# One token-mixer layer with a mixture of experts on one core: the SSM branch's projections and its scan put into one block, with the early chunk states among the gate-z items

## The chip, the cores and the metric

The kernel runs on one core of a Trainium2 chip, as one launch. The metric is the device time in microseconds. The kernel before was timed in three runs: 2568.36, 2576.6 and 2577.54 us, median 2576.6. One further execution was profiled; the rows below come from it.

## The reference, cut to what matters

The layer modulates its input, projects it into four branches, merges them behind gates, and ends with a mixture of experts. The change touches the second branch, a state-space model (SSD) with 12 heads in 4 groups, over 1024 tokens in 8 chunks of 128, plus 256 context tokens in 2 chunks, in both directions:

```
z, xbc, dt = split(p_b)                        # 768, 1792 and 24 columns of u @ w_in
xs, b_in, c_out = split(silu(conv3(xbc)))      # 768, 4 x 128, 4 x 128
dt = softplus(dt + bias);  log_decay = -dt * exp(a_log)
a_cum = cumsum(log_decay) in each chunk
decay_to_end = exp(a_cum[-1] - a_cum)
state[c] = sum_l b_in[l] * decay_to_end[l] * (xs*dt)[l]       # one per chunk and direction
h[c+1] = exp(a_cum[-1]) * h[c] + state[c]                     # the context's states start it
y = (c_out b_in^T * decay) (xs*dt) + c_out h[c] * exp(a_cum) + ssd_d * xs
y = rms_norm(y * silu(z))
```

Eleven of the chunk states are called early: four of the two context chunks (both directions), which give the initial states, and seven of the forward direction. The scan proper then walks the chunks from the last to the first, forms the backward states on its way, and writes y.

## The kernel before, in words

The program is a row of stages; each is one block in which the five engines run their own instruction lists and meet through semaphores, and each ends in a barrier of all engines (`stage`, line 361). `ssd_scan_stages` (L944) runs two of them, `stage_ssd_project` (L956) and `stage_scan` (L1302). A tensor `merged` serves as scratch in the first, and holds the forward states and then y in the second.

**Projections.** 21 items stream through a ring of four weight buffers: item 0 gives the raw dt, items 1 to 14 the xbc channels, items 15 to 20 the gate z, 128 channels each. For each item ScalarE rounds the weights and VectorE forms the remainder (`split_weights`, L924: L937 and L940). TensorE then runs `project`: 48 matmuls of 512 columns (L390; three products for each of 8 slices of the contraction and 2 halves of the tokens), into PSUM banks 0 and 1 for even items, 3 and 4 for odd ones; items up to 10 also do the context, into bank 2 or 5. After project(m), TensorE transposes the tile of item m-1 to token order (`turn`, L1112, banks 6 and 7), ScalarE evicts that (L1141), and POOL stores it to HBM: xs and b to `xbc_tok`, z to `z_tok` (L1039). b and c go out by channel as well (`xbc_chan`, L1287), and the cumulative sums to `cum_rows` (L1291). SP's queue carries the ring's loads, and behind them the stores of the last two z items. The block ends when every store has landed.

**Scan.** SP loads xs and b of each early state from `xbc_tok` (L1376, L1377), in four buffers; POOL multiplies xs by dt_to_end (L1403, "ending"); TensorE forms the state in 4 products of 192 columns (`chunk_state`, L1439; 8 records in the trace) into banks 3 and 4 or 5 and 6 in turn; VectorE decays the running state (L1566) and adds the new one (L1569). Then TensorE starts on chunk 7: `segments` (L1460, L1461; six for each chunk, banks 0, 1 and 7) give the exponents, ScalarE takes their exponentials (`grow`, L1537), VectorE mixes them with the scores of b and c (L1576, L1581), and TensorE sums skip term (L1474), diagonal term (L1482) and the states' products (`states_out`, L1468, banks 5 and 6). Each chunk also forms the backward state that the next one needs.

What sets the order: each engine's list is in program order, and a wait holds everything behind it. POOL's and SP's transfers are issued in that order too.

Of the kernel before, what the change touches and what calls it, by code (L numbers as in the profile page):

```python
# [943 lines left out]
def ssd_scan_stages(k, merged):  # L944


    with ExitStack() as ctx:
        sb = k.resident(ctx)
        n = CHUNKS + CTX_CHUNKS
        dt = {name: sb("dt_" + name, [P, n, 2, HEADS]) for name in  # L950
              ("exp_cum", "dt_to_end", "total", "bias")}
        stage_ssd_project(k, dt, merged)
        stage_scan(k, dt, merged)


def stage_ssd_project(k, dt, scratch):  # L956

# [9 lines left out]
    n = CHUNKS + CTX_CHUNKS  # L967
# [12 lines left out]
    with k.stage("xbc") as (sb, sem):  # L980
        turned = sb("turned", [P, 2, n, P])
        upper = sb("upper", [P, 2, KT * P], F32R)
        uc = sb("uc", [P, KT, CTX])
        uc_rest = twin(nc, "xbc_uc", [P, KT, CTX])
        uc_upper = sb("uc_upper", [P, KT, CTX], F32R)
        raw = sb("raw", [H2, n * P])
        bias, a_log = sb("bias", [P, H2]), sb("a_log", [P, H2])
        tmp, neg = sb("tmp", [P, n, H2]), sb("neg", [P, n, H2])
        step, log_decay, log_step, to_end, cum = (sb(x, [P, n, 2, HEADS]) for x in (
            "step", "log_decay", "log_step", "to_end", "cum"))  # L990
        cum_up, cum_lo = sb("cum_up", [CUMS, 2, P], F32R), sb("cum_lo", [CUMS, 2, P], F32R)
# [12 lines left out]
        def banks(m):  # L1004
            return 3 * (m % 2)

# [20 lines left out]
        def wide(row):  # L1027
            return row[:, :].unsqueeze(1).broadcast_to([P, n, H2])
# [4 lines left out]
        def chunks_of(v):  # L1033
            return v.rearrange("p (c h) -> p c h", c=n)
# [7 lines left out]
        raw_turned_at = ps[:, 6, 0:n * H2]  # L1042
        cum_at = [ps[:, 7, d * n * HEADS:(d + 1) * n * HEADS] for d in range(2)]
        total_at = ps[:, 7, n * H2:2 * n * H2]

        with nc.Block() as block:
            @block.sync
            def _(sp):
                sp.dma_start(uc[:, :, :], a["ctxT"].rearrange("(k p) t -> p k t", p=P)).then_inc(uc_in, 16)
                sp.dma_start(bias[:, :], k.row("dt_bias")).then_inc(small_in, 16)  # L1050
                sp.dma_start(a_log[:, :], k.row("a_log")).then_inc(small_in, 16)
                ring.stream(sp)
# [9 lines left out]
            def _(pe):  # L1062
# [18 lines left out]
                def turn_raw():  # L1081
                    pe.wait_ge(raw_ready, 2)
                    for c in range(n):
# [18 lines left out]
                def turn(m):  # L1102
# [8 lines left out]
                    for c in range(CHUNKS):  # L1111
                        mm = nc.tensor.transpose(ps[:, 6 + c // 4, (c % 4) * P:(c % 4 + 1) * P],  # L1112
                                                 shaped[:, m % 2, c * P:(c + 1) * P], k.const("ident"))
# [6 lines left out]

                for m in range(items):
# [9 lines left out]
                turn(items - 1)  # L1131

            @block.scalar
            def _(act):
# [39 lines left out]
                for m in range(1, items):  # L1174
# [26 lines left out]
                    else:  # L1201
                        free_shaped(m)
                        nc.scalar.activation(shaped[:, b, 0:T], both, ACT.Silu).then_inc(shaped_ready, 1)
# [4 lines left out]
                        if turns(m - 1):  # L1208
                            evacuate_turned(m - 1)
                evacuate_turned(items - 1)  # L1210

            @block.vector
            def _(v):
# [42 lines left out]

                for m in range(1, items):
                    if is_conv(m):
                        convolve(m)
                    if m + 2 < items:  # L1260
# [19 lines left out]
                ch.wait()  # L1280

            @block.gpsimd
            def _(pool):
                for m in range(1, items - 2):
                    if 6 < m <= convs:
                        pool.wait_ge(shaped_ready, m)
                        pool.dma_start(a["xbc_chan"][m - 7], shaped[:, m % 2, 0:T]).then_inc(chan_out[m % 2], 16)  # L1287
                    if m == turning + 3:
                        pool.wait_ge(cum_split, 2)
# [2073 lines left out]
```

## Time and profile before

| | |
|---|---|
| median of three timed runs | 2576.6 us (2568.36 to 2577.54) |
| profiled execution | 2572.02 us, span 2570.2 us |
| busy share of the span | PE 94%, PE weight loads 76%, DVE 63%, ACT 37%, POOL 10% |
| mean granted TensorE clock | 0.968 |
| projections of the SSM branch | 491 to about 792 us of the span |
| seam up to the first segments matmul | about 792 to 837 us |
| scan proper | 837 to 938 us |

PE is TensorE's matmuls, PEld its weight loads, DVE VectorE, ACT ScalarE, POOL GpSimd, SPq the transfers that SyncE issues. L1112 is line 1112 of the kernel before. A share is a mean over stages with different limits; the chain of waits of the whole execution holds only its last instruction, so the seam is read from the stretches and the timeline.

### The profile page before, as it was taken

The numbers are of one execution on the slowest core, as the hardware profiler recorded it, in microseconds if no ns is written. First come the engines' busy times: TensorE is split into PE (matmuls) and PEld (weight loads), VectorE is DVE, ScalarE is ACT, GpSimd is POOL, SyncE is SP. The second block draws the span as 40 slices with busy tenths as digits, with TensorE's granted clock in tenths as the row PEclk, the third lists the DMA queues.
The fourth block names the chain that finished last, engine by engine and source line by source line (L and its number), as shares of the span: only waits on it lengthen the run. The fifth ranks groups of instructions, "written<-read, shape, count | busy, mean of one in ns | idle before, by whom it ended". The sixth has DMA issues, their size and how long they took to land. (4 is left out here: it accounts for less than half of the span.)

```text
span 2570.2 us, 30487 instructions
## 1 busy us (share of the span) xinstructions
PE 2407.5 (94%) x11928; PEld 1950.9 (76%) x11928; DVE 1630.3 (63%) x1666; ACT 941.3 (37%) x1100; POOL 251.7 (10%) x234
## 2 busy tenths in 40 slices
PE   6999899799996989999999999999599999999994
PEld 2468778678885878788877888868588888888882
DVE  6453299533323763522984635668888889888976
ACT  5233301333321533101112100021277777777764
POOL 0000000000103310000000001100011212121210
PEclk8999999899998999999999999999799999999997
DMA  5431255212326222111111113533689999999975
GB/s 202 169 115 50 74 173 178 85 54 82 123 69 195 88 64 98 61 49 51 46 41 45 37 49 130 198 142 130 259 316 368 365 363 363 363 371 387 384 269 204
DMA packets 95120, 437.51 MB, mean 170 GB/s; under 512 B 16057, under 2 KB 28617, under 8 KB 80299
## 3 DMA queue, kind: packets, MB, share of 16 engines
q1 hardware_dynamic: 68330, 357.81, 37.5%
q0 software_dynamic: 26688, 78.30, 8.7%
q8 instruction: 70, 1.15, 0.2%
q14 instruction: 32, 0.25, 0.0%
HBM read 401.51 MB, written 55.51 MB: 178 GB/s over the span
## 5 line engine op out<-in xcount | busy, mean ns | idle before, releaser
L390 PE MATMUL ps<-uT_upper_rest,ring_rest 128*128 128x512 f32 x1296 | 513.0, 396 | 0.0
L390 PE MATMUL ps<-uT_upper_rest,mix_upper 128*128 128x512 f32 x768 | 307.6, 400 | 9.6 <-DVE mix_val L2342 5.3
L390 PE MATMUL ps<-uT_rest,mix_upper 128*128 128x512 f32 x768 | 306.5, 399 | 0.0
L390 PEld LDWEIGHTS ps<-uT_upper_rest,ring_rest 128*128 128x128 f32 x1296 | 244.8, 189 | 61.5
L390 PEld LDWEIGHTS ps<-uT_upper_rest,mix_upper 128*128 128x128 f32 x768 | 145.7, 190 | 47.1 <-DVE mix_val L2342 5.7
L390 PEld LDWEIGHTS ps<-uT_rest,mix_upper 128*128 128x128 f32 x768 | 145.7, 190 | 32.6 <-issue 0.5
L1774 ACT ACTIVATE mix_gates<-ps 128x1024 f32<-128x1024 f32 x24 | 24.7, 1027 | 384.3 <-PE ps L390 367.1
L1825 DVE TENSOR_TENSOR mix_prod<-mix_gates,ps 128x1024 f32<-128x1024 f32 x24 | 29.3, 1220 | 209.9 <-PE ps L390 209.9
L2873 PE MATMUL ps<-ex_u_raw_rest,uT_rest 128*128 128x256 f32 x560 | 157.5, 281 | 0.0
L390 PE MATMUL ps<-uT_upper_rest,xbc_upper 128*128 128x512 f32 x336 | 136.6, 407 | 7.6 <-DVE ring_rest L940 7.6
L2871 PE MATMUL ps<-ring_rest,uT_rest 128*128 128x256 f32 (+1 forms) x416 | 135.5, 326 | 3.1 <-DVE uT_rest L3236 2.4
L2871 PE MATMUL ps<-ex_upper,uT_rest 128*128 128x256 f32 (+1 forms) x424 | 135.4, 319 | 0.0
L390 PE MATMUL ps<-uT_rest,xbc_upper 128*128 128x512 f32 x336 | 135.0, 402 | 0.0
L2872 PE MATMUL ps<-ex_upper,uT_rest 128*128 128x256 f32 (+1 forms) x424 | 134.3, 317 | 0.0
L2872 PE MATMUL ps<-ring_rest,uT_rest 128*128 128x256 f32 (+1 forms) x416 | 133.5, 321 | 0.0
L2761 POOL DMA_INDIRECT y_rows<-sb_uT,ex_scatter_at x35 | 92.1, 2630 | 293.4 <-ACT sb_uT L2990 293.1
L390 PE MATMUL ps<-mix_y_upper,mix_upper 128*128 128x512 f32 x288 | 114.6, 398 | 1.8 <-DVE mix_y_bT_rest L398 1.8
L390 PE MATMUL ps<-mix_y_upper,ring_rest 128*128 128x512 f32 x288 | 112.3, 390 | 0.0
L2873 PE MATMUL ps<-uT_upper_rest,uT_rest 128*128 128x512 f32 x280 | 110.8, 396 | 0.0
L2873 PE MATMUL ps<-merged_rest,ex_hid_up 128*128 128x512 f32 x280 | 110.2, 394 | 0.0
L2873 PEld LDWEIGHTS ps<-ex_u_raw_rest,uT_rest 128*128 128x128 f32 x560 | 105.4, 188 | 0.0
L2357 DVE SCALAR_TENSOR_TENSOR mix_y_aT<-mix_val,sb_cols,mix_y_aT 128x64 f32<-128x64 f32 (+14 forms) x120 | 90.2, 752 | 4.1
(464 smaller groups left out, 5535.7 us busy)
## 6 DMA issues: line engine op xcount, KB each, us to landing
sb_spare<-in_ex_g SPq DMA_DIRECT2D x35, 2048.0 KB, 9.9
ex_u_raw<-in_ex_u SPq DMA_DIRECT2D x35, 2048.0 KB, 10.2
sb_merged<-in_ex_d SPq DMA_DIRECT2D x35, 2048.0 KB, 9.3
ring<-in_conv SPq DMA_DIRECT2D x32, 512.0 KB, 3.3
ring<-in_w_gate SPq DMA_DIRECT2D x32, 512.0 KB, 3.3
mix_piece<-in_w_late POOLq DMA_DIRECT2D x32, 512.0 KB, 5.4
ring<-in_w_ssd SPq DMA_DIRECT2D x21, 512.0 KB, 3.2
ring<-in_w_mod SPq DMA_DIRECT2D x16, 512.0 KB, 4.2
```

The source lines that it names most:

```text
L390: last = self.nc.tensor.matmul(out, weight, x[:, k, lo:hi], start=(k == 0 and n == 0), stop=(k == kt - 1 and n == 2))
L1774: nc.scalar.activation(gate_of(i), both(gate_bank(i)), ACT.Sigmoid).then_inc(gate_ready, 1)
L1825: nc.vector.tensor_tensor(mine if first else prod[:, :], gate_of(i), both(gate_bank(i) + 2), ALU.mult).then_inc(prod_ready, 1)
L2357: ins = nc.vector.scalar_tensor_tensor(out=acc[:, lo:hi], in0=val[:, t, lo + s * GRID_W:hi + s * GRID_W], scalar=weight, in1=acc[:, lo:hi] ...
L2761: pool.indirect_dma_start(out=a["y_rows"], out_offset=bass.IndirectOffsetOnAxis(scatter_at[:, i:i + 1], 0), in_=y, in_offset=None, bounds_ ...
L2871: nc.tensor.matmul(out, left_up, w_up, start=first, stop=False)
L2872: nc.tensor.matmul(out, left_lo, w_up, start=False, stop=False)
L2873: return nc.tensor.matmul(out, left_up, w_lo, start=False, stop=last)
```

## The change

The two stages become one, `stage_ssd`, with one block. Its tiles lie at chosen byte offsets of one arena of 73,344 bytes a partition, because the scan's tiles now exist beside those of the projections: tiles of the scan lie over tiles that an earlier step has done with, and waits guard the reuse. The silu of z goes to a tile of its own, since the scratch is wanted for states. `grow_b` and `off` lie partly over `turned`, from which the z stores read.

The eleven early states run inside the z items, two in each of items 15 to 19 and one in item 20 (`early_at`), in banks 2 and 5, which only items with context use. There is one pair of banks and two buffers for the loads, in place of two pairs and four. TensorE runs the first of a pair between project(m) and the turn, the second behind the turn. VectorE reads the two halves by two instructions. POOL, no longer SP, issues the loads of the early states, of chunk 7 (`state_first`) and of its b and c (`out_first`).

In chunk 0 of the scan (n = 0), ScalarE's fifth `grow`, VectorE's second `take_off` and POOL's skip product wait for `last_out`, the stores of the last two z items. SP loads chunk n = 1 and on, behind those stores. Exp's table is loaded between ScalarE's last two evictions. The scan's loop is otherwise the same.

```diff
+    FIRST = 11
+    ARENA = 73344
+        def shaped_of(m):
+            return shaped[:, m % 2, 0:T] if is_conv(m) else shaped_z[:, m % 2, :]
...
+        grow_f, grow_b = at_byte("grow_f", 0, [P, 2, HEADS, P]), at_byte("grow_b", 12288, [P, HEADS, P])
+        off, skip = at_byte("off", 18432, [P, SSD_D]), at_byte("skip", 21504, [P, SSD_D])
+        xs, xend = at_byte("xs", late, [P, 2, SSD_D]), at_byte("xend", late + 6144, [P, 2, SSD_D])
...
+        def early_sum(h):
+            return ps[:, 2 + 3 * h, 0:half]
+
+        def early_at(m):
+
+            return range(max(2 * (m - convs - 1), 0), min(2 * (m - convs), FIRST))
...
             @block.sync
...
+                for n in range(1, CHUNKS):
+                    if n == 1:
+                        sp.wait_ge(state_mm, last_early(1) + 1)
+                        chan_done(sp)
+                    else:
+                        sp.wait_ge(y_done, n - 1)
+                    load_state(sp, n % 2, chunk(n), in_state[n % 2])
+                    load_out(sp, n, in_out[n % 2])
...
             @block.tensor
...
+                def early_state(m):
+                    if m:
+                        pe.wait_ge(state_read, 2 * m)
+                    pe.wait_ge(in_early[m % 2], 32 * (m // 2 + 1))
+                    chunk_state(m, m % 2, early_sum)
                 for m in range(items):
                     project(m)
...
+                    for e in early_at(m)[:1]:
+                        early_state(e)
                     if m >= 2 and turns(m - 1):
                         turn(m - 1)
+                    for e in early_at(m)[1:]:
+                        early_state(e)
                 pe.wait_ge(ring.freed, ring.done(base + items - 1))
                 pe.sem_inc(ring.freed, full - items)
                 turn(items - 1)
...
+                pe.wait_ge(rounded, 4)
+                segments(0, 0)
+                segments(0, 1)
+                pe.wait_ge(turned_ready, reads_until(items - 1) + 2)
+                segments(0, 2)
+                forward_out(0)
...
             @block.scalar
...
+                nc.scalar.preload_act_table(ACT.Exp)
                 evacuate_turned(items - 1)
+                act.wait_ge(dt_ready, 1)
+
+                def grow(n, u):
+                    act.wait_ge(seg_mm, 6 * n + u + 1)
+                    if n == 0 and u == 4:
+                        act.wait_ge(last_out, 32)
...
             @block.vector
...
+                def early_state(m):
...
+                    v.wait_ge(state_mm, m + 1)
+                    for h in range(2):
+                        tt(as_halves(new)[:, h, :], as_halves(new)[:, h, :], early_sum(h), ALU.add).then_inc(state_read, 1)
+                    v.wait_ge(state_read, 2 * (m + 1))
...
                 for m in range(1, items):
                     if is_conv(m):
                         convolve(m)
+                    for e in early_at(m):
+                        early_state(e)
+                    if m == convs + 2:
+                        prepare()
                     if m + 2 < items:
                         split_weights(k, None, v, base, m + 2, upper, cast, w_split)
...
+                    take_off(n, 0, state_in(c))
+                    mix(n, 0)
+                    if n:
+                        take_diagonal(n - 1)
+                    if n == 0:
+                        v.wait_ge(last_out, 32)
+                    take_off(n, 1, off[:, :])
...
             @block.gpsimd
...
+                def early_ready(m):
+
+                    for e in early_at(m):
+                        if e >= 2:
+                            pool.wait_ge(state_mm, e - 1)
+                        load_state(pool, e % 2, early[e][1], in_early[e % 2])
+                    for e in early_at(m):
+                        pool.wait_ge(in_early[e % 2], 32 * (e // 2 + 1))
+                        ending(e % 2, early[e][1], early[e][0])
...
                     elif convs < m < items - 2:
+                        early_ready(m + 1)
                         store_z(pool, m, tok_out[turn_no(m) % 2])
+                    if m == turning + 3:
+                        pool.wait_ge(dt_ready, 1)
+                        for b in range(2):
+                            pool.wait_ge(tok_out[b], 16 * (turning // 2))
+                        early_ready(convs + 1)
+                    if m == convs + 1:
+                        chan_done(pool)
+                        load_out(pool, 0, out_first)
+                        pool.wait_ge(blank, 1)
+                        load_rows(0, 0)
+                        load_rows(0, 1)
+                early_ready(items - 1)
+                pool.wait_ge(state_mm, FIRST)
+                load_state(pool, 0, chunk(0), state_first)
...
+                    else:
+                        pool.wait_ge(d_in, 16)
+                        pool.wait_ge(last_out, 32)
```

## Rows read from the trace of the kernel before

**Rows 1.** Stretches: us, then each engine's busy time, granted clock, DMA share, GB/s.

```profile
779.00:792.00 13.00, 13.00 (x64) 10.64 (x63) 0.00 (x0) 2.41 (x4) 0.89 (x1) 1.00 0.14 40
792.00:798.00 6.00, 1.60 (x13) 1.15 (x11) 0.00 (x0) 2.87 (x5) 0.00 (x0) 1.00 0.81 237
798.00:804.00 6.00, 0.00 (x0) 0.00 (x0) 0.11 (x1) 0.14 (x1) 0.00 (x0) 0.51 0.64 200
804.00:810.80 6.80, 0.00 (x0) 0.00 (x0) 2.05 (x3) 1.64 (x3) 1.47 (x1) 0.50 0.74 243
810.80:837.00 26.20, 18.50 (x88) 15.93 (x88) 21.19 (x21) 0.00 (x0) 18.38 (x12) 0.92 0.90 297
```

**Rows 2.** Timeline of PE over the seam: start, duration, instruction, idle before and releaser.

```profile
791.49 1.04 PE L1112 MATMUL ps<-sb_consts,sb_merged 128*128 128x128 f32 x8
794.10 1.06 PE L1112 MATMUL ps<-sb_consts,sb_merged 128*128 128x128 f32 x8 [1.57 <-ACT xbc_turned L1141]
810.86 5.03 PE L1439 MATMUL ps<-scan_xend,scan_b_tok 128*128 128x192 f32 x16 [15.69 <-POOL scan_xend L1403]
...
837.31 0.36 PE L1460 MATMUL ps<-scan_never,scan_eye 128*128 128x256 f32 x1 [2.60 <-DMA scan_rows<-cum_rows]
...
838.82 1.47 PE L1468 MATMUL ps<-sb_merged,scan_c_chan 128*128 128x192 f32 x8
```

**Rows 3.** Timeline of PE, one z item earlier: turn and next projection.

```profile
779.42 1.03 PE L1112 MATMUL ps<-sb_consts,sb_merged 128*128 128x128 f32 x8
780.21 0.48 PE L390 MATMUL ps<-uT_upper_rest,xbc_upper 128*128 128x512 f32 x1
```

**Rows 4.** Timelines of DVE and POOL in the z items.

```profile
769.82 1.23 DVE L940 TENSOR_TENSOR ring_rest<-ring,xbc_upper 128x1024 fp32r<-128x1024 f32 x1 [10.85 <-ACT xbc_upper L937]
782.18 0.89 POOL L1039 DMA_DIRECT2D z_tok<-xbc_turned  x1 [10.23 <-ACT xbc_turned L1141]
```

**Rows 5.** Timelines of DVE and PE: evictions, and a chunk state inside the scan.

```profile
703.88 0.41 DVE L1273 CAST xbc_cum_up<-ps 96x256 fp32r<-96x256 f32 x1
...
846.02 1.52 PE L1439 MATMUL ps<-scan_xend,scan_b_tok 128*128 128x192 f32 x8
847.24 0.41 PE L1460 MATMUL ps<-scan_never,scan_eye 128*128 128x256 f32 x1
847.65 0.95 DVE L1612 TENSOR_TENSOR scan_state_b<-scan_state_b,ps 128x768 f32<-128x768 f32 x1 [1.21 <-PE ps L1439]
```

**Rows 6.** A POOL transfer, POOL's products (min/median/max ns), landing of b.

```profile
715.72 0.53 POOL L1287 DMA_DIRECT2D xbc_chan<-sb_merged  x1 [10.86 <-ACT sb_merged L1199]
...
L1403 POOL TENSOR_TENSOR scan_xend<-scan_xs,sb_dt_dt_to_end x13: 1462/1470/2181, 809.2 to 917.1; 128x768 f32<-128x768 f32 x13
...
DMA to landing us min/median/max: 3.3/3.7/6.2
```

**Rows 7.** ACT's last eviction and table load; the last z stores, and their landing.

```profile
795.20 1.07 ACT L1141 COPY xbc_turned<-ps 128x512 f32<-128x512 f32 x2 [1.25 <-PE ps L1112]
...
804.38 1.28 ACT L1537 ACT_TABLE_LOAD   x1
...
793.98 2.69 SPq L1039 DMA_DIRECT2D z_tok<-xbc_turned  x2
...
z_tok<-xbc_turned SPq DMA_DIRECT2D x2, 512.0 KB, 6.8
```

**Rows 8.** Chunk 0 of the scan: POOL's skip product, PE's use of it.

```profile
839.84 1.50 POOL L1427 TENSOR_TENSOR scan_skip<-scan_xs,scan_d_row 128x768 f32<-128x768 f32 x1
843.74 0.81 PE L1474 MATMUL ps<-scan_skip,sb_consts 128*128 128x384 f32 x2
```

**Rows 9.** The stage after: a stretch at the lower clock, and two matmuls in it.

```profile
941.00:944.50 3.50, 3.29 (x8) 2.62 (x9) 3.43 (x6) 0.00 (x0) 0.00 (x0) 0.50 0.30 102
...
942.23 0.63 PE L390 MATMUL ps<-uT_upper_rest,ring_rest 128*128 128x512 f32 x1
942.65 0.63 PE L390 MATMUL ps<-uT_upper_rest,mix_upper 128*128 128x512 f32 x1
```

More of the change, by code:

```diff
@@ L1027, in wide @@
         def wide(row):
-            return row[:, :].unsqueeze(1).broadcast_to([P, n, H2])
+            return row[:, :].unsqueeze(1).broadcast_to([P, n_all, H2])
         def heads(v):
@@ new lines, in halves, with as_halves, last_early, chan_done @@
+        def halves(first_bank):
+            return ps[:, first_bank:first_bank + 2, 0:half]
+        def as_halves(v):
+            return v.rearrange("p (b n) -> p b n", b=2)
+        def last_early(b):
+            return max(m for m in range(FIRST) if m % 2 == b)
+        def early_sum(h):
+            return ps[:, 2 + 3 * h, 0:half]
+        def early_at(m):
+            return range(max(2 * (m - convs - 1), 0), min(2 * (m - convs), FIRST))
+        def chan_done(eng):
+            for b in range(2):
+                eng.wait_ge(chan_out[b], 16 * sum(q % 2 == b for q in range(7, convs + 1)))
@@ new lines, in load_state, with load_out @@
+        def load_state(eng, b, c, landed):
+            eng.dma_start(xs[:, b, :], a["xbc_tok"][c, :, 0:SSD_D]).then_inc(landed, 16)
+            eng.dma_start(b_tok[:, b, :], a["xbc_tok"][c, :, SSD_D:SSD_D + GROUPS * P]).then_inc(landed, 16)
+        def load_out(eng, n, landed):
+            c = chunk(n)
+            for q, dst in enumerate((b_chan, c_chan)):
+                src = a["xbc_chan"][GROUPS * q:GROUPS * (q + 1), :, c * P:(c + 1) * P]
+                eng.dma_start(dst[:, n % 2, :, :], src.rearrange("g p t -> p g t")).then_inc(landed, 16)
@@ L1131, in _, with segments @@
                 turn(items - 1)
+                def segments(n, u):
+                    at_bank = SEG[(6 * n + u) % 3]
+                    if 6 * n + u >= 3:
+                        pe.wait_ge(grown, 6 * n + u - 2)
+                    pe.wait_ge(in_rows[u // 3], 16 * (n + 1))
+                    for d in range(2):
+                        out = ps[:, at_bank, d * PAIR:(d + 1) * PAIR]
+                        nc.tensor.matmul(out, eye[:, :], never[:, d, :], start=True, stop=False)
+                        mm = nc.tensor.matmul(out, ones[:, :], rows[:, d, u * PAIR:(u + 1) * PAIR], start=False, stop=True)
+                    mm.then_inc(seg_mm, 1)
@@ new lines, in states_out, with skipped @@
+                def states_out(n, d):
+                    b = n % 2
+                    state = state_in(chunk(n)) if d == 0 else state_b[:, b, :]
+                    for g in range(GROUPS):
+                        mm = nc.tensor.matmul(ps[:, 5 + g // 2, (g % 2) * 192:(g % 2 + 1) * 192],
+                                              c_chan[:, b, g, :], state[:, g * 192:(g + 1) * 192], start=True, stop=True)
+                    mm.then_inc(off_mm, 1)
+                def skipped(n, q):
+                    pe.wait_ge(skip_ready, n + 1)
+                    nc.tensor.matmul(ps[:, 3 + q, 0:half], k.const("ident"), skip[:, q * half:(q + 1) * half],
+                                     start=True, stop=False)
@@ new lines, in diagonal @@
+                def diagonal(n, q):
+                    pe.wait_ge(mixed, 2 * n + q + 1)
+                    pe.wait_ge(in_state[n % 2] if n else state_first, 32 * max((n + 1) // 2, 1))
+                    for e in range(6):
+                        h = 6 * q + e
+                        mm = nc.tensor.matmul(ps[:, 3 + q, e * HD:(e + 1) * HD], grow_f[:, n % 2, h, :],
+                                              xs[:, n % 2, h * HD:(h + 1) * HD], start=False, stop=(e == 5))
+                    mm.then_inc(diag_mm, 1)
@@ L1571, in _ @@
+                        ch.wait()
+                        v.sem_inc(dt_ready, 1)
                 v.sem_inc(state_done, 1)
```

460 lines of the change are left out of this document (184 added, 276 removed).

## The prediction

> **What bounds the kernel now.** I read the stretches first (busy time of every engine and the clock granted to TensorE, stretch by stretch), because the page's share of 94% for PE is a mean over stages. In the seam between projections and scan that share collapses: 13.0 us of 13.0 while the last gate-z items run, then 1.60 of 6.0, 0 of 6.0, 0 of 6.8, and 18.50 of 26.2 [rows 1]. The timeline of PE names the events. The last projection gives way to the turn of z item 19 at 791.49, item 20's turn starts at 794.10, the first early chunk state at 810.86, and the scan proper (the segments matmul) only at 837.31 [rows 2]. So 45.8 us lie between the end of the projections and the scan, with 20.1 us of PE work in them. Inside the z items PE is saturated and the others wait: one item costs 12.07 us, of which its turn costs 0.79 [rows 2, 3], while DVE stood idle 10.85 us before its one split and POOL 10.23 us before its one store [rows 4]. The early states would lie beside idle engines, but on the engine that has no idle.
>
> **The change part by part.** Let T be the end of a z projection.
>
> *PE work moved into the z items.* An early chunk state occupies PE's queue for 1.22 us (846.02 to 847.24), its last result comes out at 847.54 and DVE starts on it at 847.65 [rows 5]. All eleven now use one pair of banks, so the next one waits until DVE has read both halves. No row has a 384-column eviction; 256 columns took 0.41 us and 768 took 0.95 [rows 5], so I estimate 0.55 each, 1.1 for the two, and the next state starts 2.8 us after the one before. Items 16 to 19 put a turn into that gap: 2.8 + 1.22 = 4.0 us, less the 0.8 for the turn which was there before, is 3.2 us each, 12.8 together. Item 15 has no turn in the gap: 4.0. Item 20 has one state: 1.2. Sum 18.0 us. If the gap cost nothing it would be 11 x 1.22 = 13.4; I keep that as the low end.
>
> *Does POOL deliver in time?* POOL must store z item m-1, issue four loads, and form two products before T of the next item. From T: first state and turn 2.0, eviction of the turn some 1.5 more, so the store starts at T + 3.6. Then 0.9 for the store [rows 4] and 4 x 0.55 for the loads (POOL issued a plain transfer of 128 rows in 0.53 [rows 6]), landing 3.7 us after issue (SP's loads of the same rows; POOL's own have no row yet), products 1.47 each [rows 6]: the first is ready about T + 10.8, the second T + 12.3. PE asks for them at T + 15.2 and T + 18.0. With the worst rows (0.89 an issue, landing 6.2, product 2.18) it is about T + 14.7 and T + 16.8, still in time. One item is tighter: on item 16 POOL also loads the first b and c blocks, waits for DVE to clear the rows tile and issues two row loads, some 4 us more. Mean rows still fit, the worst rows cost about 4 us. I take zero and keep 7 us (this item, and one us for each of three others) as the high end. DVE's added work, some 4 us of 15 per item, lies before its next weight split, which PE needs an item later; cover gone, each us would be a us. The ring's loads stay on SP's queue; the early loads add 640 KB a state, about 87 GB/s over a 15 us item, where the seam ran 237 GB/s and more [rows 1].
>
> *The end of the z phase.* With 18.0 us more, item 19's turn starts at 809.5 and item 20's at 812.1; the first two segments follow at once, at 812.9. Before, this was 837.31: a lead of 24.4. The third segment needs the bank of item 20's turn. ScalarE evicted that one from 795.20 [rows 7], now 813.2; the activation table load of 1.28 us [rows 7] is put between its two evictions, where ScalarE waited for PE 1.25 us anyway, so the eviction ends at 814.4 (0.1 late). The first forward product follows at 814.9 against 838.82 [rows 2]: the lead is 23.9.
>
> The Trainium skill, "ScalarE: Activation LUTs", section "What ACT_TABLE_LOAD costs", adds a drain of about 1.38 us to each switch; by it the eviction and the rest would come 1.4 us later and the gain would be 18.1 instead of 19.5. No row separates such a drain.
>
> *The wait that replaces the barrier.* The tiles of the scan now share bytes with the buffer from which z is stored, so ScalarE's fifth pair of growth factors, DVE's second off-diagonal product and POOL's skip product of chunk 0 wait until the last two z stores have landed. Behind POOL's wait stand the skip product, the next end product and a row load; PE waits for the first two. Before, the two stores were issued from 793.98 to 796.67 and took 6.8 us [rows 7], and the barrier opened right behind them. Now the second goes out at 814.4; 6.8 makes 821.2, and I add 1.5 (an estimate) because the loads of chunk 7 and 6 share the DMA engines: 822.7. The skip product (1.50 [rows 8]) ends at 824.2. PE used it at 843.74 [rows 8], 19.5 us later. The end product follows by 1.5, at 825.7, and PE comes to the state that needs it 2.28 us after the skip (843.74 to 846.02 [rows 5, 8]), at 826.5: no further loss. From here the eight chunks run as before, since their code and waits are the same. The loads of chunk 6, which went out well ahead before, now go out behind the z store at about 815 and land some 6 us later; they are wanted about 828. The lead that counts is therefore **19.5 us**. If the stores land in 3.8 us, the lead stays 23.9; 4 us later than I take, it is 15.5.
>
> What else changes (arrays laid over each other, more semaphores cleared at the stage's end, two small ScalarE copies on item 16) lies beside PE or is below 1 us; the clear I bound by 0 and 1.
>
> **The sum.** The profiled execution took 2572.0 us; less 19.5 it is 2552.5. The median shown is 2576.6, 4.6 above it, and the three runs (2568.4 to 2577.5) lie on both sides, so I go half way: **2555 us**. Its own range: a z phase longer by only 13.4 would give a lead of 24.1, a landing 4 us later 15.5, the clear one less, 14.5. From a base of 2574.5, give or take 2.3, that is 2548 to 2562.
>
> **The rivals.**
>
> *POOL is late: the early states do not hide.* POOL's queue is in order, and each pair of loads waits behind a store that itself waits for PE. For it: in the seam PE waited 15.69 us for POOL's first product [rows 2], and everything now sits in this queue. Against: over 4 us of slack by typical rows. With 7 us lost, the lead is 12.5 and the time 2562; with landings still slower (10 us each pair) it loses 4 us an item, about 20, and nothing is left: 2574. Range of this rival 2562 to 2574. One way to get there: products took up to 2.18 us beside DVE instead of 1.47 [rows 6]; if the store, the two loads and the product ahead of a first state each waited out one DVE instruction of 1.23 us [rows 4], that state would be ready at T + 15.7, half a us late, 2 us over four items. The Trainium skill, "SBUF — State Buffer", section "SBUF: two separate sides", gives the rule for it: GpSimd, which also writes the descriptors of POOL's transfers, is locked out for the whole of a DVE instruction in a two-port mode or with two SBUF inputs. The trace agrees for the products; for transfers no row shows it. It is why this case has more than a tenth.
>
> *The seam's wait is bigger than the barrier was.* Here it decides only how much is gained: a landing 12 us after issue, at 826.4, ends the skip product at 827.9, a lead of 15.8 and 2559. It is inside the forecast's range.
>
> *TensorE's clock falls in the z items; slower.* Today the z items run unbroken at 1.00. The seam shows 0.51 and 0.50 after PE had stopped [rows 1], the lower of the two levels (1.2 and 2.4 GHz). At that level (granted 0.50 in 941.0 to 944.5) one 512-column matmul follows another after 0.42 us (942.23 to 942.65 [rows 9]) against 0.235 (12.07 less 0.79 us for the 48 of an item [rows 2, 3]): 9 us an item. The breaks that I forecast are 0.8 us, in item 15 1.6. If they pull the clock down, the five items behind cost 45 us more and the time is 2600; the point from which the change loses is a little over two items at the low clock. Against: with PE busy 1.60 us of 6 the granted clock was still 1.00 [rows 1]. The Trainium skill names this pattern in "TensorE: Matmul & The Clock Gate", section "HAM oscillation — how this bites in real kernels": waits between bursts of matmuls re-throttle the array. The row of 792 to 798 does not bear it out for breaks this short.
>
> **How the numbers follow.** Forecast 0.72, POOL late 0.16, low clock 0.05, something slower that I do not see 0.03, a lead above 25 us 0.04. About 0.5% (12.9 us) is what a measurement of this kernel can tell from no change. Faster by more than that holds the forecast, the large lead and the edge of the POOL case: 0.77. Within it: 0.15. Slower: 0.08. A range of 2544 to 2568 leaves out about a fifth.
>
> **What would show it.** In the new profile: z items of about 15.2 us spacing, PE near full and clock 1.00 through them; the early states' matmuls between the projections; the first segments right behind the last turn; one idle stretch of PE, up to 5 us, in chunk 0 in front of the skip matmul, ended by POOL; about 100 us from chunk 0 to the scan's end, as before. Wrong would be: PE waiting in the z items for POOL's products by more than 1 us an item, granted clock under 1.00 there, or a seam with PE idle over 10 us.

## The result, and the profile after

The changed kernel took 2553.6 us (median of five runs, 2547.15 to 2556.08); the kernel before, on the same chip, 2573.45 us (five runs, 2568.36 to 2577.54). The ratio is 0.9918, its 95% interval 0.9898 to 0.9937. The forecast was 2555 us, 2544 to 2568. The profiled executions have spans of 2551.1 and 2570.2 us.

The same stretches, read in the changed kernel (times in us from the span's start; then each engine's busy time, the granted clock, DMA share and GB/s):

```profile
734.00:805.00 71.00, 68.59 (x331) 57.34 (x330) 25.91 (x36) 13.80 (x19) 29.52 (x34) 1.00 0.45 136
...
812.00:816.00 4.00, 2.49 (x21) 2.08 (x19) 1.68 (x3) 3.46 (x6) 1.04 (x2) 1.00 1.00 330
...
818.50:821.60 3.10, 3.10 (x25) 2.97 (x23) 2.47 (x3) 1.71 (x7) 0.00 (x0) 1.00 1.14 349
821.60:824.40 2.80, 0.07 (x1) 0.00 (x0) 1.55 (x2) 1.52 (x7) 1.44 (x1) 0.91 1.09 379
824.40:828.30 3.90, 3.82 (x14) 3.21 (x15) 0.84 (x1) 0.65 (x3) 2.74 (x3) 0.50 0.17 44
828.30:830.80 2.50, 2.50 (x11) 2.50 (x10) 0.00 (x0) 0.00 (x0) 0.00 (x0) 0.51 0.02 7
830.80:836.00 5.20, 5.20 (x40) 4.93 (x39) 4.80 (x6) 3.20 (x12) 0.66 (x2) 1.00 0.01 2
```

The first row is the z items: PE is busy but for 2.41 of 71 us, at full clock. The 24.9 us without PE work between 792 and 837 [rows 1] are gone. In their place are a stop of 1.25 us between the last two turns and one of 2.8 us, and behind the second stand 6.4 us of the scan's first chunk at the low clock, where the kernel before ran at 1.00 (its own low stretch lay ahead of the scan, in the seam [rows 1]).

The timeline of PE in one z item (two early states and the turn between them), and then in the seam (start, duration, instruction, idle before and releaser; L1212 is the chunk state, L1200 the turn, L1247 the segments, L1261 the skip term, L1269 the diagonal term):

```profile
764.39 1.46 PE L1212 MATMUL ps<-ssd_xend,ssd_b_tok 128*128 128x192 f32 x8
765.69 1.04 PE L1200 MATMUL ps<-sb_consts,ssd_shaped_z 128*128 128x128 f32 x8
767.03 1.57 PE L1212 MATMUL ps<-ssd_xend,ssd_b_tok 128*128 128x192 f32 x8 [0.31 <-DVE sb_merged L1483]
...
779.64 1.46 PE L1212 MATMUL ps<-ssd_xend,ssd_b_tok 128*128 128x192 f32 x8
...
811.43 1.04 PE L1200 MATMUL ps<-sb_consts,ssd_shaped_z 128*128 128x128 f32 x8
813.72 1.07 PE L1200 MATMUL ps<-sb_consts,ssd_shaped_z 128*128 128x128 f32 x8 [1.25 <-ACT ssd_turned L1319]
814.54 0.36 PE L1247 MATMUL ps<-ssd_never,ssd_eye 128*128 128x256 f32 x1
...
824.48 1.65 PE L1261 MATMUL ps<-ssd_skip,sb_consts 128*128 128x384 f32 x2 [2.81 <-POOL ssd_skip L1639]
825.92 2.66 PE L1269 MATMUL ps<-ssd_xs,ssd_grow_f 128*128 128x64 f32 x12
828.37 2.68 PE L1212 MATMUL ps<-ssd_xend,ssd_b_tok 128*128 128x192 f32 x8
830.76 0.41 PE L1247 MATMUL ps<-ssd_never,ssd_eye 128*128 128x256 f32 x1
```

A z item takes 15.25 us (764.39 to 779.64) with one stop of 0.31; four of these and one of 1.18 in item 15 make up the 2.41 us. The segments follow 3.11 us behind item 19's turn, where they followed 45.82 [rows 2]. The skip matmul waits for POOL, whose timeline names what POOL waited for, as predicted the z stores; the same view of SP shows them going out:

```profile
822.97 1.46 POOL L1639 TENSOR_TENSOR ssd_skip<-ssd_xs,ssd_d_row 128x768 f32<-128x768 f32 x1 [5.33 <-DMA z_tok<-ssd_turned]
...
813.61 2.76 SPq L1047 DMA_DIRECT2D z_tok<-ssd_turned  x2
```

To compare executions, I count from the first projection matmul of this branch (499.15 us into the span before, 501.43 after), up to the end of DVE's last add of the scan (938.06 before, 920.00 after), which I call the scan's end. The lines of both, the kernel before first:

```profile
499.15 0.79 PE L390 MATMUL ps<-uT_upper_rest,xbc_upper 128*128 128x512 f32 x1 [7.63 <-DVE ring_rest L940]
...
937.11 0.95 DVE L1594 TENSOR_TENSOR sb_merged<-sb_merged,ps 128x768 f32<-128x768 f32 x1 [1.72 <-PE ps L1482]
```

```profile
501.43 0.80 PE L390 MATMUL ps<-uT_upper_rest,ssd_upper 128*128 128x512 f32 x1 [7.62 <-DVE ring_rest L940]
...
919.05 0.95 DVE L1550 TENSOR_TENSOR sb_merged<-sb_merged,ps 128x768 f32<-128x768 f32 x1 [1.71 <-PE ps L1269]
```

The lead of the changed kernel is then 25.1 us at the first segments (338.16 less 313.11), 21.5 at the skip matmul (344.59 less 323.05), 18.8 at chunk 1's first segments (348.09 less 329.33), and 20.3 at the scan's end (438.91 less 418.57). The stage behind starts 20.1 earlier; from there to the end it took 1.3 less, and the branch's first matmul came 2.3 later. Together 19.1, the difference of the spans. The last two are no part of the change: over all the kernels here, the first matmul came at 494.3 to 501.9 and the stages behind took 1627.6 to 1630.5.

### The profile page after: what moved, and what is told of

Read it like the earlier page. It is cut to its first block and busy times, and to the rows that moved or that the text cites. A ratio compares the mean times of both kernels' runs of the same rounds, so it can differ in the third digit from the quotient of the medians.

```text
span 2551.1 us, 30480 instructions
## 1 busy us (share of the span) xinstructions
PE 2408.1 (94%) x11928; PEld 1950.2 (76%) x11928; DVE 1630.2 (64%) x1677; ACT 941.2 (37%) x1100; POOL 269.4 (11%) x260
## 5 line engine op out<-in xcount | busy, mean ns | idle before, releaser
L390 PE MATMUL ps<-uT_upper_rest,ssd_upper 128*128 128x512 f32 x336 | 136.8, 407 | 7.6 <-DVE ring_rest L940 7.6
L390 PE MATMUL ps<-uT_rest,ssd_upper 128*128 128x512 f32 x336 | 134.9, 402 | 0.0
```

The costliest lines, as they stand in the source:

```text
L390: last = self.nc.tensor.matmul(out, weight, x[:, k, lo:hi], start=(k == 0 and n == 0), stop=(k == kt - 1 and n == 2))
```

## Experiments

Median and ratio are against the kernel before on the same chip. Three such groups of runs were made (before: 2569.14, 2572.4 and 2572.51 us); one more kernel was run once. By time most of these kernels cannot be told from the changed one, since the intervals of their ratios overlap; what tells them apart are the traces.

**Undo the hiding: all early states behind the last projection, in the one block without a barrier.**

```diff
-            return range(max(2 * (m - convs - 1), 0), min(2 * (m - convs), FIRST))
+            return range(FIRST) if m == items - 1 else range(0)
...
                         load_state(pool, e % 2, early[e][1], in_early[e % 2])
...
+                        if e:
+                            finish(e - 1)
```

> The changed kernel in one block, without the early states beside the z items: all eleven run at item 20, behind the last projection, POOL loading two ahead as in the change. Theory (the gain is the hiding of loads and products behind the projections; the block alone gives little): z items back to 12.07 us, then some 42 us for eleven states (two in about 7.6 us: loads 1.1 and 3.7 us to land, product 1.5, state 1.5), with PE mostly waiting and its clock low; first segments about where they were before the change, time 2570 to 2582. Rival (the dropped barrier and the waits around it, 792 to 810 before the change, are most of the gain): the seam shrinks by some 12 us, 2558 to 2563.

Measured: 2585.53 us, ratio 1.007 (1.0053 to 1.0086). PE's timeline, the first of the eleven states and two others, then POOL ahead of one:

```profile
787.56 1.47 PE L1212 MATMUL ps<-ssd_xend,ssd_b_tok 128*128 128x192 f32 x8
...
802.18 2.90 PE L1212 MATMUL ps<-ssd_xend,ssd_b_tok 128*128 128x192 f32 x8 [3.08 <-POOL ssd_xend L1579]
808.15 2.90 PE L1212 MATMUL ps<-ssd_xend,ssd_b_tok 128*128 128x192 f32 x8 [3.08 <-POOL ssd_xend L1579]
```

```profile
799.41 0.58 POOL L1116 DMA_DIRECT2D ssd_xs<-xbc_tok  x1 [2.84 <-PE ps L1212]
...
800.53 1.50 POOL L1579 TENSOR_TENSOR ssd_xend<-ssd_xs,sb_dt_dt_to_end 128x768 f32<-128x768 f32 x1
```

The time is above the range that I gave. The states follow each other mostly every 5 to 6 us, not the 3.8 of my sum. In this run POOL's list has the load for the next state ahead of a product; that load waits for an earlier state, and the product stands behind it (it starts as the load's issue ends, with no wait for its own data). I had also named the low clock but priced a state at 1.5 us; at the low clock one takes 2.9. So one block with the states behind the projections, in this order and with two buffers, loses.

The run does not show that the missing barrier alone gives nothing. Its first state started 20.6 us earlier than in the kernel before (291.12 us after the first projection matmul against 311.71), because its loads had gone out at 780.24, with no barrier to hold them back. From that state to the first segments it took 57.5 us, where the kernel before took 26.5. One block with four buffers and the states behind the projections was not run, so that rival is open.

**Undo the other part: the hiding stays, PE waits for the z stores before the scan.**

```diff
                 pe.wait_ge(rounded, 4)
+                pe.wait_ge(last_out, 32)
                 segments(0, 0)
```

> The changed kernel with one wait more: TensorE waits for the last two z stores ahead of the first segments, as it did behind the barrier of the kernel before; the early states stay among the z items. Theory (the hiding is the gain, the missing barrier is worth only what the stores' landing would hold up in chunk 0 anyway): first segments at 321 to 322 us after the first projection matmul instead of 313.1, skip matmul at 328 to 331 instead of 323, chunk 1's first segments at 331 to 335 instead of 329.3, and the time 2 to 6 us above the changed kernel, still 13 us or more below the kernel before. Rival (each us of the landing counts in full): 8 us or more above the changed kernel.

Measured: 2555.24 us, ratio 0.9936 (0.9923 to 0.995); the changed kernel on the same chip 2551.06, 0.9918 (0.9903 to 0.9934). PE and the stretches:

```profile
822.24 0.55 PE L1247 MATMUL ps<-ssd_never,ssd_eye 128*128 128x256 f32 x1 [7.76 <-issue]
...
821.00:824.00 3.00, 1.76 (x8) 1.79 (x9) 0.00 (x0) 0.46 (x2) 0.00 (x0) 0.50 1.09 377
824.00:827.00 3.00, 3.00 (x13) 3.00 (x12) 0.00 (x0) 2.74 (x11) 1.54 (x2) 0.50 0.19 47
827.00:830.00 3.00, 3.00 (x25) 3.00 (x24) 2.50 (x3) 1.16 (x5) 1.96 (x2) 1.00 0.03 8
```

Against the changed kernel on the same chip the segments come 8.0 us later (321.10 from the first matmul), chunk 1's first segments only 3.6 (332.89), the scan's end 3.4 (421.83). The stores hold up chunk 0 either way; what this wait takes away is the work that PE can do ahead of the skip term. So with the hiding in place some 4 us of the gain hang on PE not waiting for the stores, and the rest, 17 us by the medians (2572.4 less 2555.24), stays when it does wait. Only PE waits here, while the old barrier held every engine.

**Take the wait away: chunk 0 needs the store of item 19 only.** Item 20's turned tile gets bytes of its own, so nothing of chunk 0 lies over it. The growth factors and the `off` tile then wait for item 19's store, and the skip product, whose tile lay over item 20's (byte 21504 of the arena), for neither of the last two.

```diff
+        turned_last = at_byte("turned_last", 8192, [P, CHUNKS, P])
...
-                    store_z(sp, m, last_out)
+                    store_z(sp, m, last_out if m == items - 1 else next_out)
...
-                        pool.wait_ge(last_out, 32)
+                        pool.wait_ge(tok_out[1], 16 * len(turn_order[:-2][1::2]))
```

> The changed kernel, but item 20's turned tile goes to the bytes 8192 to 12287, so that growth factors and the second off-diagonal product of chunk 0 wait for item 19's store alone, the skip product for no z store of the last two, and item 20's store is waited for at chunk 1. Theory (the gate on the last store costs PE 2.8 us of idle time before the skip matmul, and the clock that falls in it some 2.8 us more up to the next segments): the skip matmul comes within 1 us of the segments before it, granted clock 1.00 through chunk 0, the scan ends 4 to 5.5 us earlier, about 2549 us. Rival (the skip product is late for its own reason, chunk 7's xs being loaded only after the last early state): PE waits at the same place for over 2 us, and the time stays at about 2553.5. Second rival (it is regained later in the scan, as the changed kernel regained 1.6 us between its chunk 0 and its last): earlier by 4 us at chunk 1, by under 2 at the end, 2552.

Measured: 2548.9 us, ratio 0.9919 (0.9903 to 0.9936): by time not to be told from the change. The trace:

```profile
764.74 1.54 PE L1217 MATMUL ps<-ssd_xend,ssd_b_tok 128*128 128x192 f32 x8 [0.73 <-POOL ssd_xend L1586]
...
821.92 0.84 PE L1266 MATMUL ps<-ssd_skip,sb_consts 128*128 128x384 f32 x2
...
823.88 1.52 PE L1217 MATMUL ps<-ssd_xend,ssd_b_tok 128*128 128x192 f32 x8
```

PE goes into the skip term with no stop, the chunk state takes 1.52 us and not 2.68, and the scan ends at 414.65 us instead of 418.57, 3.9 us earlier, just under the 4 to 5.5 expected. At chunk 1's first segments it is 5.1 us, 6.1 if counted from the first segments: the stop of 2.8 and the low clock behind it. Two things gave some back: the first segments came 1.0 us later here (item 17 waited 0.73 us for POOL), and the scan behind chunk 1 took 1.2 us longer, with one wait of 1.82 us for a c block. The second rival of the expectation, that the gain is given back later in the scan, holds for that part.

**Keep the wait, keep TensorE busy in it.** Seven spare matmuls, whose bank the skip term overwrites.

```diff
+                    if n == 0 and q == 0:
+                        for _ in range(7):
+                            nc.tensor.matmul(ps[:, 3, 0:half], k.const("ident"), k.consts[:, 0:half], start=True, stop=True)
                     pe.wait_ge(skip_ready, n + 1)
```

> The changed kernel with seven extra 384-column matmuls into a free bank (their results are overwritten) right ahead of the wait for the first skip product: PE works through the stretch in which it waited 2.8 us. Theory (the matmuls behind the wait ran at half clock because PE had stopped: skip 1.65 instead of 0.81 us, diagonal 2.66 instead of 1.55, state 2.68 instead of 1.52): granted clock 1.00 through chunk 0, these three back at 0.81, 1.55 and 1.52 us, the skip matmul no earlier (or up to 0.5 us later, if the fillers outlast the wait), the segments of chunk 1 about 2.5 us earlier relative to it; the kernel about 2551. Rival (they were long because of data: products of POOL and DVE late, DMA): no change in them, 2553.5 or slower by the fillers.

Measured: 2548.57 us, ratio 0.993 (0.9912 to 0.9949). Stretches of the filled kernel:

```profile
815.00:820.00 5.00, 5.00 (x21) 3.37 (x20) 2.83 (x3) 2.17 (x8) 3.00 (x2) 1.00 0.93 307
820.00:823.00 3.00, 3.00 (x20) 2.51 (x19) 0.00 (x0) 0.00 (x0) 1.17 (x2) 1.00 0.04 10
```

```profile
820.42 0.81 PE L1264 MATMUL ps<-ssd_skip,sb_consts 128*128 128x384 f32 x2
...
823.57 0.41 PE L1247 MATMUL ps<-ssd_never,ssd_eye 128*128 128x256 f32 x1
```

At clock 1.00, from the skip matmul to chunk 1's segments takes 3.15 us instead of 6.28: 3.1 us is the price of the low clock. The spare work outlasted the wait by 1.9 us (the skip product was done at 818.46), so the skip matmul came 0.8 us later than in the changed kernel, more than the 0.5 that I allowed, and chunk 1's segments 2.4 earlier. Of these 1.4 us is left at the scan's end; in this run one wait for c took 1.50 us. The time cannot tell that from nothing; the records can.

**Double POOL's work on the early states.**

```diff
+                    if early:
+                        nc.gpsimd.tensor_tensor(by_head(xend[:, b, :]), by_head(xs[:, b, :]),
+                                                per_head(at("dt_to_end", c, d)), ALU.mult).then_inc(xend_once, 1)
```

> The changed kernel with POOL's product of each early state done twice (same values): 1.47 us and a hand-over more for each, on POOL alone. Theory (POOL has slack except in item 17, where its products were ready 0.5 and 0.9 us before PE asked): item 17 about 2 to 2.5 us longer, the other z items unchanged within 0.3, total 2 to 3 us slower, 2556. Rival (POOL's chain sets the pace of the z items): each of the five pairs 3 us longer, 15 us in all, 2568.

Measured: 2550.68 us, ratio 0.9928 (0.9911 to 0.9945). PE's stops for POOL in the z items are two, both in item 17:

```profile
763.14 1.54 PE L1213 MATMUL ps<-ssd_xend,ssd_b_tok 128*128 128x192 f32 x8 [0.84 <-POOL ssd_xend L1585]
766.12 1.54 PE L1213 MATMUL ps<-ssd_xend,ssd_b_tok 128*128 128x192 f32 x8 [0.57 <-POOL ssd_xend L1585]
```

Eleven products of 1.47 us more, 16 us of POOL's time, cost about 1.3 of PE's, less than the 2 to 3 expected. The hiding has slack everywhere but in the item for which POOL also fetches the scan's first blocks.

**Spread the states otherwise: one in item 15, two in each of 16 to 20.**

```diff
-            return range(max(2 * (m - convs - 1), 0), min(2 * (m - convs), FIRST))
+            return range(max(2 * (m - convs) - 3, 0), min(max(2 * (m - convs) - 1, 0), FIRST))
```

> The changed kernel with the eleven early states spread otherwise: one in item 15 and two in each of items 16 to 20. Theory (a second state costs its hand-over only where no turn fills the gap): item 15 loses its stop of 1.2 us and one state of 1.2 to 1.5 us, and item 20 gets a state that falls mostly into the time in which TensorE waited for item 19's eviction. The first segments come 2 to 2.5 us earlier after the first projection matmul (310.5 to 311.2 instead of 313.1), everything behind them as much earlier, and the time is 1.5 to 3 us below the changed kernel. Rival: chunk 7's loads, which wait for the last early state, become what the skip product waits for; then the segments come 2 us earlier and the skip matmul does not, and the time is within 0.5 us of the changed kernel.

Measured: 2548.56 us, ratio 0.9905 (0.9888 to 0.9922), and the changed kernel beside it:

> The changed kernel once more, as the mark for the other kernels on this chip. Both theories: 18 to 29 us below the kernel before (ratio 0.989 to 0.993), the same stop of TensorE of 2.5 to 3.1 us in front of chunk 0's skip matmul, granted clock about 0.5 behind it, chunk state 2.5 to 2.9 us.

2551.06 us, 0.9918 (0.9903 to 0.9934). The segments come 2.4 us earlier (310.71), as expected; the scan's end 4.5 (413.94), because here the clock did not fall:

```profile
821.60 0.91 PE L1261 MATMUL ps<-ssd_skip,sb_consts 128*128 128x384 f32 x2 [2.55 <-POOL ssd_skip L1639]
...
823.84 1.54 PE L1212 MATMUL ps<-ssd_xend,ssd_b_tok 128*128 128x192 f32 x8
```

**Does an earlier, shorter stop tip the clock?** The kernel just told has no stop of 1.25 us between the last two turns. Two spare matmuls there in the changed kernel, run once:

```diff
+                for _ in range(2):
+                    nc.tensor.matmul(ps[:, 3, 0:half], k.const("ident"), k.consts[:, 0:half], start=True, stop=True)
                 turn(items - 1)
```

> The changed kernel with two spare 384-column matmuls between the turns of z items 19 and 20, in the 1.25 us in which TensorE waits there for ScalarE; the stop of some 2.8 us in front of the skip matmul stays. Two runs differ so far with nearly the same stop: 2.55 us with the clock at 1.00 behind it (the shifted early states, which have no such earlier stop), 2.58 us and more with 0.50. Theory (the earlier stop of 1.25 us is what tips it): granted clock 1.00 behind the stop, skip matmul 0.8 to 0.95 us, chunk state 1.5 us, chunk 1's first segments 326 to 327 us after the first projection matmul instead of 329.3. Rival (it is chance or the place of the last stop alone): clock 0.50 behind the stop, skip matmul 1.6 us, chunk 1's first segments at 329 to 330.

Measured: 2548.43 us, the kernel before 2573.3. PE's timeline:

```profile
820.97 0.91 PE L1263 MATMUL ps<-ssd_skip,sb_consts 128*128 128x384 f32 x2 [3.42 <-POOL ssd_skip L1641]
...
823.21 2.90 PE L1212 MATMUL ps<-ssd_xend,ssd_b_tok 128*128 128x192 f32 x8
```

The stop before the skip matmul was longer here (3.42 us); the skip matmul still took 0.91 us, but the chunk state 2.90, and chunk 1's segments came at 327.66, between the two expectations. The clock fell later, not never. Inconclusive; why a stop of 2.55 us passed without a fall stays open. More records say that neither the earlier stop nor the length of the last one decides. The kernel with the doubled product has that stop of 1.25 us, and its clock too fell only after the skip matmul (a stop of 2.67 us, skip matmul 0.91, chunk state 2.87). And the kernel before, which stopped 2.60 us ahead of its first segments [rows 2], kept its clock, while the kernel with the hiding undone lost it behind a stop of 2.23 us in the scan. The stretch behind the first of these two stops, then the second stop and a stretch behind it:

```profile
837.30:841.00 3.70, 3.69 (x29) 3.70 (x29) 1.29 (x2) 2.94 (x12) 1.71 (x2) 1.00 0.12 30
```

```profile
909.17 2.27 PE L1255 MATMUL ps<-sb_merged,ssd_c_chan 128*128 128x192 f32 x8 [2.23 <-DMA ssd_c_chan<-xbc_chan]
...
911.00:913.30 2.30, 2.30 (x9) 1.69 (x7) 1.81 (x2) 0.00 (x0) 0.00 (x0) 0.50 0.00 0
```

**All of it joined:** the wait for item 19's store only, the shifted states, the two load buffers exchanged (chunk 7's loads then wait for the tenth state), and the scan's first blocks fetched two items later (`m == convs + 3`).

> Candidate: the kernel of the earlier run in which chunk 0 waits only for item 19's store, with the shifted early states, the two load buffers exchanged (so that chunk 7's loads wait for the tenth early state, not the eleventh), and the first b and c blocks and row loads issued two items later on POOL. Theory: no POOL wait of 0.5 us or more in items 16 to 20, segments 309.5 to 311 us after the first projection matmul, skip matmul about 7 us behind them at clock 1.00, the scan's end at 410.5 to 413 us (418.6 in the changed kernel, 414.7 in the earlier run), and a time 5 to 8.5 us below the changed kernel. Rival: the scan is held by its own chunks further on, so that an earlier start is given back; then the scan's end is at 414 or later and the time not more than 4 us below.

> The joined kernel of the earlier run once more, as the mark on this chip: 5 to 8.5 us below the changed kernel's distance from the kernel before, that is a ratio of 0.987 to 0.9905; in the scan TensorE waits for the c block of every chunk, 0.3 to 1.8 us each, 4 to 6 us in all.

Measured: 2544.0 us, ratio 0.9888 (0.9872 to 0.9904), and on the next chip 2545.82, 0.9904 (0.9889 to 0.9919). The scan ends at 412.99 and 409.92; in the first of the two PE waited for c blocks 5.2 us in all, one wait of 1.70 among them, in the second 3.3, less than I expected. From chunk 1's segments to the scan's end the two differ by 1.9 us, as much as these waits do.

**The c block first.** In the scan `states_out` of each chunk from the second or third on waits for c, the last of four loads. PE's timeline, one such wait in the kernel before, and the same chunk's in the changed one:

```profile
899.70 1.57 PE L1468 MATMUL ps<-sb_merged,scan_c_chan 128*128 128x192 f32 x8 [1.60 <-DMA scan_c_chan<-xbc_chan]
```

```profile
881.40 1.57 PE L1255 MATMUL ps<-sb_merged,ssd_c_chan 128*128 128x192 f32 x8 [0.50 <-DMA ssd_c_chan<-xbc_chan]
```

The six such waits are 4.71 us before (0.40, 0.54, 0.90, 1.60, 0.43, 0.84) and 3.16 after (0.39, 0.44, 0.32, 0.50, 0.92, 0.59). That is the 1.6 us by which the lead grew again between chunk 1 and the scan's end. The test exchanges two lines of SP:

```diff
-                    load_state(sp, n % 2, chunk(n), in_state[n % 2])
                     load_out(sp, n, in_out[n % 2])
+                    load_state(sp, n % 2, chunk(n), in_state[n % 2])
```

> The changed kernel, where SyncE issues the b and c blocks of chunks 1 to 7 ahead of xs and b by token, and not behind them. Theory (the scan's chunks are paced by the landing of the c block, and that is why 1.6 us came back behind the seam): c lands 1.5 to 2.3 us earlier, TensorE's waits for it (six of 0.3 to 0.9 us, 3.2 us in all) go, chunks follow each other every 11.7 to 12.0 us, from chunk 1's first segments to the scan's end it takes 86 to 87 us (89.2 in the changed kernel), and the time falls by 2 to 3.5 us. The seam with its low clock stays. Rival (the four transfers of a chunk share the engines and land together whatever the order, or xs becomes late for the skip product): c lands less than 0.5 us earlier, or a wait of the same size stands before the skip matmul, and the time is within 1 us.

> The joined kernel with the b and c blocks issued first. Theory: its waits for c (seven of 0.4 to 1.7 us, 5.2 us in all) go, the scan from chunk 1's first segments takes 86 to 87.5 us (91.6 in the joined kernel), and the time is 3.5 to 5 us below the joined kernel, 10 to 13 below the changed kernel. Rival: as for the other kernel, within 1 us of the joined kernel.

Measured on the changed kernel: 2549.27 us, ratio 0.9904 (0.9888 to 0.9919); on the joined one 2541.26, 0.988 (0.9865 to 0.9895), beside the joined one's 2545.82. By time neither is clear of the kernel without the exchange; the scan's end is 4.8 us earlier than in the changed kernel (413.74) and 3.9 earlier than in the joined one (406.04). The issues by transfer (KB, us from issue to landing) on the changed kernel, in one chunk, first as it was and then with c first:

```profile
ssd_c_chan<-xbc_chan SPq DMA_DIRECT2D x1, 256.0 KB, 4.6
```

```profile
ssd_xs<-xbc_tok SPq DMA_DIRECT2D x1, 384.0 KB, 4.6
ssd_b_chan<-xbc_chan SPq DMA_DIRECT2D x1, 256.0 KB, 3.1
ssd_c_chan<-xbc_chan SPq DMA_DIRECT2D x1, 256.0 KB, 3.4
ssd_b_tok<-xbc_tok SPq DMA_DIRECT2D x1, 256.0 KB, 5.8
```

c was issued 1.33 us behind the chunk's first load and landed 4.6 after that; now it is 0.41 and 3.4, so 2.1 us earlier. No wait for c is left, every chunk behind the first takes 11.64 us (12.2 to 12.8 in the changed kernel), and from chunk 1's segments to the scan's end it takes 84.7 us instead of 89.2, better than I expected (in the joined kernel 84.6 instead of 89.6). The joined kernel with c first is the fastest run here, 31 us below the kernel before it and some 10 below the change, by the ratios 0.988 and 0.9918.

## Why the prediction was right, step by step

- *PE work in the z items, 18.0 us.* 17.7: item 19's turn came 310.00 us after the first matmul, 292.34 before. Two states lie 2.64 us apart (764.39 to 767.03), not 2.8, since DVE reads a half in 0.51 us; item 15, with no turn in the gap, stopped PE 1.18 us.
- *POOL delivers in time, zero.* Right, with less room than the sum had. The loads took 6.3 us to their use (769.62 to 775.94, the next item's), not 3.7, so that a first product was ready at T + 13.0 and not T + 10.8, 2.2 us ahead of PE. In item 17, for which POOL fetched the scan's first blocks as well, the room was 0.5 us. The rival of a late POOL is answered by the doubled product: it decides in one item. I had let the lock-out reach POOL's transfers beside the weight split, which has two inputs. For such an instruction the Trainium skill, "SBUF — State Buffer", section "SBUF: two separate sides", speaks only of a GpSimd operation that reads SBUF, a condition that I left out. The trace fits it: beside the split of 769.76 (1.23 us) the early loads' issues took 0.56 each; only the issue of c rose, to 1.89 us, beside a DVE clear of 2.06, which has one input.
- *The end of the z phase, a lead of 24.4 at the segments.* 25.1. The table load lies between the evictions as I put it. ACT's timeline:

```profile
813.60 1.28 ACT L1392 ACT_TABLE_LOAD   x1
814.89 1.07 ACT L1319 COPY ssd_turned<-ps 128x512 f32<-128x512 f32 x2
```

  The eviction starts as the load ends. The Trainium skill, "ScalarE: Activation LUTs", section "What ACT_TABLE_LOAD costs", adds a drain of about 1.38 us; this trace does not show one.
- *The wait that replaces the barrier, a lead of 19.5.* The place, the releaser and the order of the two POOL products were right. The landing was too late in my sum: I put it 10.6 us behind item 20's turn (812.1 to 822.7), it came 9.2 behind (813.72 to 822.97). From the second store's issue behind its eviction (815.96) it took 6.9 us, close to the 6.8 of the row; the 1.5 us that I had added for contention did not come. With the 0.7 from the z phase the lead at the skip matmul was 21.5.
- *"From here the eight chunks run as before."* This step failed, twice, and the errors in part cancel: that is luck. I had forecast an idle stretch of PE in chunk 0 and did not ask what it does to the clock; I had asked that only of the z items. The stop of 2.81 us was followed by 6.4 us at 0.50, worth 2.8 us of lead. Then 1.6 us came back, because the chunks are paced by the landing of c, whose waits happened to be shorter.
- *The low-clock rival.* In the z items it did not happen: 1.00 throughout, with stops of 0.31 and 1.18 us. The Trainium skill, "TensorE: Matmul & The Clock Gate", section "HAM oscillation — how this bites in real kernels", describes waits between bursts of matmuls that throttle the array again. I had set it aside for those short breaks; this trace agrees with it at the one longer stop, where I had not looked (2.81 us, then 0.50).
- *The sum.* 19.5 forecast, 20.1 at the next stage's start, 19.1 between the spans. The mechanism was right: the hidden states, the wait that is left, and its place. That the number is so near is in part luck. The lead at the skip matmul was 2.0 above the forecast, the low clock took 2.8, and the shorter waits for c gave 1.6.

## What to carry to other kernels

Hide a stage's preparation in a stage that PE fills: 18 us of PE time cost 18 us there and shrank a 46-us seam to 3 us, as long as the slow queue keeps ahead in its fullest item. Where a barrier is replaced by a wait, price the wait and also the clock of what follows it. And when a consumer waits for the last of several loads, issue its load first: two exchanged lines brought the scan's end 4 to 5 us forward, about as much as PE's not waiting for the stores.

## What the runs showed of the hardware

- The length of PE's stop alone did not decide whether the granted clock fell. In front of the skip matmul it fell behind stops of 2.58, 2.67, 2.75, 2.81 and 3.42 us (at 2.67 and 3.42 only after the skip matmul) and not behind one of 2.55. Elsewhere it fell behind one of 2.23 us and not behind one of 2.60. Stops of 0.2 to 1.8 us in the z items and in the scan proper were never followed by a fall. Which other thing decides stays open.
- POOL's products rose from 1.46 us to 1.91 and 2.17 in places; the issues of the early states' loads stayed at 0.54 to 0.59 through the z items. One issue, of c, took 1.89 us (754.98 to 756.87), while DVE cleared a tile for 2.06 (754.52 to 756.58). In the joined kernels, where that issue comes two items later and does not meet the clear, it took 0.75, and the clear 1.76.
- Four loads issued within 1.5 us of each other landed in the order of their issue, in the one chunk read of each kernel: 3.3 to 4.6 us after issue with c last, 3.1 to 5.8 with c second. With 1152 KB under way the order decided who waits.
